# Hybrid block: nine units' low limbs by ScalarE and adding transfers, and eleven convolution taps from TensorE to VectorE

## What is computed

```python
proj = h @ w_in                                    # 1024 -> 2560
q, k, v, u, gate = split(proj)                     # five times 512
a_out = merge_heads(stick_breaking_attention(q, k, v))   # 8 heads of 64
c = u * sigmoid(gate)                              # 512 channels
c = causal_depthwise_conv(c, dw_w, dw_b)           # y_t = sum_k w_k x_(t-30+k) + b, 31 taps
c = silu(layer_norm(c, ln_g, ln_b))
m = concatenate([a_out, c]) @ w_out                # 1024 -> 1024
```

## Time and profile before

| | us |
|---|---|
| median of 3 runs | 1420.3 |
| lowest and highest | 1419.64, 1420.34 |
| span of the profiled execution | 1417.5 |
| PE (matmul) busy in the span | 1404.2 |
| VectorE busy | 940.8 |
| ScalarE busy | 723.2 |
| POOL busy | 150.7 |

### The profile page before, as it was taken

The page is one execution under the profiler, slowest core; times in us unless marked ns, Lnnn a source line. Parts: engine busy times, 40 slices in busy tenths (PEclk is TensorE's granted clock), DMA queues, the critical chain, the costliest instruction groups (busy, mean ns, idle before and its releaser), DMA issues.

```text
span 1417.5 us, 19077 instructions
## 1 busy us (share of the span) xinstructions
PE 1404.2 (99%) x7339; PEld 1149.0 (81%) x7339; DVE 940.8 (66%) x1294; ACT 723.2 (51%) x1042; POOL 150.7 (11%) x232
## 2 busy tenths in 40 slices
PE   9999999999999999999999999999999999999998
PEld 7888888688888888888878888888877788888886
DVE  6666667886676667665786857755568666765544
ACT  6444455564443445543755645446556644654442
POOL 1600010010000000000172100000552110000000
PEclk9999999999999999999999999999999999999999
DMA  9686765256876778868544688763945355565551
GB/s 317 199 252 201 260 203 205 68 177 199 259 243 206 235 233 259 252 216 264 181 144 163 202 205 265 250 211 125 247 154 194 119 178 179 163 209 184 201 193 61
DMA packets 236346, 286.15 MB, mean 202 GB/s; under 512 B 37028, under 2 KB 160720, under 8 KB 236256
## 3 DMA queue, kind: packets, MB, share of 16 engines
q1 hardware_dynamic: 235856, 284.63, 63.1%
q10 hardware_dynamic: 400, 0.31, 0.1%
HBM read 280.70 MB, written 4.20 MB: 201 GB/s over the span
## 4 chain that ended last, share of the span: by engine, by line
PE 95%; DVE 2%; issue 1%; ACT 1%; DMA 0%; SPq 0%; POOL 0%; POOLq 0%; ACTq 0%
PE ps L583 30%; PE ps L586 29%; PE ps L584 29%; PE pst L790 1%; PE pst L949 1%; DVE wlo L475 1%; PE pst L1225 1%; PE ps L1172 0%; DMA raw<-in_ffn_w_in_dram 0%; ACT whi L466 0%; PE pst L1539 0%; PE pst L2112 0%; PE ps L1209 0%; PE ps L1689 0%; PE pst L2321 0%
## 5 line engine op out<-in xcount | busy, mean ns | idle before, releaser
L475 DVE TENSOR_TENSOR wlo<-raw,whi 128x1024 fp32r<-128x1024 f32 (+2 forms) x474 | 564.2, 1224 | 252.3 <-ACT whi L466 250.7
L466 ACT ACTIVATE whi<-raw 128x1024 fp32r<-128x1024 f32 (+2 forms) x474 | 472.3, 1040 | 233.7 <-PE ps L586 94.0
L583 PE MATMUL ps<-whi,xh 128*128 128x512 f32 (+2 forms) x1438 | 563.9, 392 | 1.8 <-ACT xh L829 0.8
L584 PE MATMUL ps<-wlo,xh 128*128 128x512 f32 (+2 forms) x1438 | 553.6, 385 | 0.0
L586 PE MATMUL ps<-whi,xl 128*128 128x512 f32 (+2 forms) x1438 | 545.1, 385 | 0.0
L583 PEld LDWEIGHTS ps<-whi,xh 128*128 128x128 f32 x1438 | 270.0, 188 | 61.9 <-issue 4.7
L586 PEld LDWEIGHTS ps<-whi,xl 128*128 128x128 f32 x1438 | 270.0, 188 | 54.9
L584 PEld LDWEIGHTS ps<-wlo,xh 128*128 128x128 f32 x1438 | 270.2, 188 | 51.0
L583 PE MATMUL ps<-whi,gh 128*128 128x512 f32 x440 | 172.0, 391 | 0.0
L584 PE MATMUL ps<-wlo,gh 128*128 128x512 f32 x440 | 171.2, 389 | 0.0
L586 PE MATMUL ps<-whi,gl 128*128 128x512 f32 x440 | 153.4, 389 | 0.0
(11 more groups left out here) (272 smaller groups left out, 894.2 us busy)
## 6 DMA issues: line engine op xcount, KB each, us to landing
raw<-in_ffn_w_in_dram SPq DMA_DIRECT2D x174, 512.0 KB, 5.4
raw<-in_ffn_w_out_dram SPq DMA_DIRECT2D x40, 1024.0 KB, 5.8
raw<-in_w_in_dram SPq DMA_DIRECT2D x26, 1024.0 KB, 5.1
adat<-in_w_ada_dram SPq DMA_DIRECT2D x96, 256.0 KB, 3.1
raw<-in_w_ffn_gate_dram SPq DMA_DIRECT2D x22, 512.0 KB, 4.1
raw<-in_w_ffn_up_dram SPq DMA_DIRECT2D x22, 512.0 KB, 5.1
raw<-in_hyb_w_in_dram SPq DMA_DIRECT2D x10, 1024.0 KB, 5.2
raw<-in_gla_w_in_dram SPq DMA_DIRECT2D x10, 1024.0 KB, 5.1
```

What stands on the lines that cost most here:

```text
L466: e.activation(split_of(whi, j), raw_of(j), ACT.Copy).then_inc(*whi_made.up(j))
L475: e.tensor_tensor(split_of(wlo, j), raw_of(j), split_of(whi, j).bitcast(F32), ALU.subtract).then_inc(*wlo_made.up(j))
L583: e.matmul(ps[:, 0:n], a, whi_of(j, k), start=first and k == 0, stop=False)
L584: last = e.matmul(ps[:, 0:n], a, wlo_of(j, k), start=False, stop=False)
```

## The change

Units 5 to 13 of the hybrid stage (subs +10 to +27, 18 subs) are "soft". For them VectorE no longer makes the low limb. ScalarE writes the high limb as before and then the same value negated into `wlo` (a second activation with scale -1); POOL waits for that and issues a transfer that reads the same weights from DRAM again and adds them to `wlo`. TensorE and the loads of SP wait for that transfer (`s_lo`) instead of `wlo_made`. TensorE's taps are now the 31 of block 3, VectorE's the 93 of blocks 0 to 2; the added sum of block 2 is gone, and the copy, the join and the final read of the crossed quadrants are 256 columns wide instead of 512. The counts in the hand-written orders change with it.

```diff
+        soft = [*range(U0[1] + 5, U0[2])]
+        def lo_ready(j):
+            return s_lo[j % NSPL].at(j) if subs[j][0] in soft else wlo_made.at(j)
...
             if i >= NRAW:
-                e.wait_ge(*wlo_made.at(last_sub[i - NRAW]))
+                if i - NRAW in soft:
+                    e.wait_ge(*lo_ready(first_sub[i - NRAW]))
+                e.wait_ge(*lo_ready(last_sub[i - NRAW]))
...
                 e.activation(split_of(whi, j), raw_of(j), ACT.Copy).then_inc(*whi_made.up(j))
+                if u in soft:
+                    e.activation(split_of(wlo, j), raw_of(j), ACT.Copy, scale=-1.0).then_inc(*neg_made.up(j))
...
-                e.wait_ge(*whi_made.at(j))
-                e.tensor_tensor(split_of(wlo, j), raw_of(j), split_of(whi, j).bitcast(F32), ALU.subtract
-                                ).then_inc(*wlo_made.up(j))
+                if u not in soft:
+                    e.wait_ge(*whi_made.at(j))
+                    e.tensor_tensor(split_of(wlo, j), raw_of(j), split_of(whi, j).bitcast(F32), ALU.subtract
+                                    ).then_inc(*wlo_made.up(j))
...
+        def pool_lo(e, st):
+            for j in range(J0[st], J0[st + 1]):
+                u, k, m, n = subs[j]
+                if u in soft:
+                    srcs = plan[u][0]
+                    e.wait_ge(*neg_made.at(j))
+                    if len(srcs) == 1:
+                        e.dma_start(split_of(wlo, j), srcs[0][0][:, k:k + m, :], accum_op=ALU.add
+                                    ).then_inc(*s_lo[j % NSPL].up(j))
...
             if tok == 0:
-                e.wait_ge(*wlo_made.at(j))
+                e.wait_ge(*lo_ready(j))
...
-        NT = 20
-        PE_TAPS = [(2, k) for k in range(NT, 31)] + [(3, k) for k in range(31)]
-        TAPS = [(b, k) for k in range(31) for b in range(3) if b < 2 or k < NT]
+        PE_TAPS = [(3, k) for k in range(31)]
+        TAPS = [(b, k) for k in range(31) for b in range(3)]
...
-                t = e.matmul(tb.of("conv")[q, :], ident[p, p], hid[1][p, 0:512], start=False, stop=True,
+                t = e.matmul(tb.of("conv")[q, 0:256], ident[p, p], hid[1][p, 0:256], start=False, stop=True,
...
-            e.activation(hid[1][:, 0:512], tb.of("convx")[:, :], ACT.Copy).then_inc(*convx_made.up())
+            e.activation(hid[1][:, 0:256], tb.of("convx")[:, 0:256], ACT.Copy).then_inc(*convx_made.up())
...
             pool_open(e, 1)
+            pool_lo(e, 1)
             pool_open(e, 2)
```

More of the change, by code:

```diff
@@ L171, in program @@
         s_out_act = sig("s_out_act", 16)
+        s_lo = [sig(f"s_lo{i}", 16) for i in range(NSPL)]
+        neg_made = sig("neg_made")
         whi_made = sig("whi_made")
@@ L482, in split_lo @@
                         ada_sum(e, ada_summed[u])
+        def pool_lo(e, st):
[7 more added lines that the diff above has]
+                                    ).then_inc(*s_lo[j % NSPL].up(j))
+                    else:
+                        e.dma_start(split_of(wlo, j), raw_of(j), accum_op=ALU.add).then_inc(*s_lo[j % NSPL].up(j))
         def ada_add(e, c, k):
@@ L1059, in program @@
         tap_made = sig("tap_made")
-        taps_joined = sig("taps_joined")
         scored = sig("scored")
@@ L1215, in pe_taps @@
                 if i == 0:
-                    for name, last in ((("conv",), [(taps_joined,), (conv_out,)]), (("convx",), [(convx_made,)])):
+                    for name, last in ((("conv",), [(conv_out,)]), (("convx",), [(convx_made,)])):
                         tb.next(name, *last)
@@ L1224, in pe_taps @@
                     q = slice(64 - p.start, P - p.start) if i % 2 else p
-                    t = e.matmul(ps[q, (b - 2) * 256:(b - 1) * 256], diag[p, i * 64:(i + 1) * 64], cx_of(b, k)[p, :],
+                    t = e.matmul(ps[q, 0:256], diag[p, i * 64:(i + 1) * 64], cx_of(b, k)[p, :],
                                  start=i < 2, stop=i % 2 == 1 and k >= 29, skip_group_check=True)
@@ L1261, in pair @@
                     step(e, hd)
-            pe_taps(e, PE_TAPS[0:10])
+            pe_taps(e, PE_TAPS[0:8])
             pair(pe_weights, 0)
-            pe_taps(e, PE_TAPS[10:18])
+            pe_taps(e, PE_TAPS[8:14])
             pair(pe_weights, 1)
@@ L1267, in pe_hyb @@
             pe_scores(e, 2)
-            pe_taps(e, PE_TAPS[18:24])
+            pe_taps(e, PE_TAPS[14:18])
             pair(pe_values, 1)
             pe_scores(e, 3)
-            pe_taps(e, PE_TAPS[24:30])
+            pe_taps(e, PE_TAPS[18:22])
             pair(pe_weights, 2)
-            pe_taps(e, PE_TAPS[30:36])
+            pe_taps(e, PE_TAPS[22:26])
             pair(pe_weights, 3)
-            pe_taps(e, PE_TAPS[36:42])
+            pe_taps(e, PE_TAPS[26:31])
             pair(pe_values, 2)
@@ L1282, in norm @@
                     pe_total(e, "mean", y_of,
-                             lambda b: conv_out.at() if b == 3 else taps_joined.at() if b == 2
-                             else tap_made.at(b, 30), (y_centred, 3))
+                             lambda b: conv_out.at() if b == 3 else tap_made.at(b, 30),
+                             (y_centred, 3))
                 if i == 2:
@@ L1337, in act_hyb @@
             e.wait_ge(*conv_dot.at())
-            e.activation(hid[1][:, 0:512], tb.of("convx")[:, :], ACT.Copy).then_inc(*convx_made.up())
+            e.activation(hid[1][:, 0:256], tb.of("convx")[:, 0:256], ACT.Copy).then_inc(*convx_made.up())
             act_values(e, 2)
             e.wait_ge(*conv_sum.at())
-            e.activation(y_of(3), tb.of("conv")[:, 256:512], ACT.Identity, bias=vector("cb", 3)).then_inc(*conv_out.up())
+            e.activation(y_of(3), tb.of("conv")[:, 0:256], ACT.Identity, bias=vector("cb", 3)).then_inc(*conv_out.up())
             act_values(e, 3)
@@ L1396, in dve_hyb @@
                     if c > 2 or i >= 2:
-                        some(3)
+                        some(5)
             def logs(g):
@@ L1404, in dve_hyb @@
             logs(1)
-            some(20)
+            some(16)
             logs(2)
@@ L1410, in dve_hyb @@
             dve_values(e, 1)
-            some(11)
+            some(8)
             dve_values(e, 2)
             some(len(TAPS))
-            e.wait_ge(*tap_made.at(2, NT - 1))
-            e.wait_ge(*conv_out.at())
-            e.tensor_tensor(y_of(2), tb.of("conv")[:, 0:256], y_of(2), ALU.add).then_inc(*taps_joined.up())
             dve_values(e, 3)
```

## The result

The changed kernel takes 1434.05 us (median; 1434.02 to 1434.19), beside 1420.26 us before: a ratio of 1.0098, 95% interval 1.0084 to 1.0112. It is slower, as forecast, but by 13.8 us and not by 3.9. The profiled spans differ by 14.7 us (1417.5 and 1432.2): what lies around the span is 1.8 us in all four executions of the changed kernel, where the forecast took over the 2.8 us of the kernel before.

The account below looks back on a forecast made before the run. PE's matmul count and whatever makes PE wait bound the kernel. Taps and join -2.8, DVE free sooner -0.1, stall +4.7, clock +2.1 give +3.9 us: 1424.2 us, range 1419.3 to 1428.5.

Parts of the forecast that it names:

- PE's gain: Convolution taps and join on PE: 44 fewer tap matmuls save 2.37 us, the narrower join 0.42, 2.8 us in all.
- VectorE: Last taps before the layer norm's first total: done near 281.5 us, in time for PE at 281.6; cost 0, bound 1.0.
- sub +27: In w_out, the negated value is ready only 1.3 us before PE begins this sub, so PE stalls 4.7 us (1.8 to 7.7).
- L: Time for POOL to issue an adding transfer and for it to land: 1.0 + 5.0 = 6.0 us, bounds 3.1 and 9.
- the clock: After the 4.7 us stall, PE's granted clock falls to half rate for about 4 us, losing 2.1 us (bounds 0 and 4).
- Rival (a): The stall before sub +27 comes without a fall of the clock: +1.8 us, 1422.1 us; chance 0.24.
- room for 9 MB more: Hybrid stage: DMA shares of 0.53, 0.16 and 0.22 in three stretches leave space for the added reads of weights.
- no other wait of PE over 0.5 us: Sign of being right: from 215 us to the 4.7 us wait before sub +27, PE has no other wait this long.
- ScalarE's own cost at 0: A second activation per soft sub, 0.97 us each on ScalarE, delays nothing PE needs, so it costs 0.
- (c): Slow transfer, adding at a lower rate than copying: L = 8.5 us, stall 7.2 us, clock down, +6.4 us, 1426.7 us; chance 0.18.
- (b): Quick transfer, adding costs nothing: L = 4.1 us, stall 2.8 us, clock stays, -0.1 us, 1420.2 us; chance 0.15.
- (d): The new chain of negated value and adding transfer is hidden after all, so PE's gain stands: 1417.4 us; chance 0.06.

Follow-up runs that it names:

- the taps alone: Changed kernel with no soft unit: VectorE makes all low limbs as before and does the 93 taps as well; 1416.12 us, ratio 0.9974.
- the last unit alone: Changed kernel with only one soft unit, the last (subs +26 and +27); 1423.20 us, ratio 1.0021.
- the copying kernel: Changed kernel whose eighteen POOL transfers copy the weights over the negated values and add nothing, so its output differs; 1420.72 us, ratio 1.0007.
- three late units: Changed kernel with only three soft units, subs +20 to +25, whose low limbs are needed latest; 1416.37 us, ratio 0.9978.

## Why the prediction was wrong

**Right: PE's gain.** Forecast 2.8 us off PE and 0.1 beside it; the marked stretches give 2.8, and the taps alone shorten the profiled span by 3.1 us (1417.5 to 1414.4). The medians differ by 3.8 us, with an interval of 2.3 to 5.1 us about it; part of that lies around the span.

**Right: VectorE.** The last taps were to end near 281.5 us with PE at the total at 281.6; in the kernel with the taps alone, 281.5 and 281.49.

**Right: sub +27.** L alone was to be 6.0 us, and was 5.8; the wait was to be 4.7 us, and was 4.7 in the changed kernel and 4.7 alone. POOL's part is 1.20 us an issue, where I took 1.0; the two small errors in L (POOL's part too low, the rest too high) cancel in part. Taking that unit out gave 6.0 us.

**Right: the clock.** It fell, for 3.4 us where about 4 were forecast, at a price of 1.9 us in the profiled executions of the changed kernel and of the one with the last unit alone, against 2.1. Rival (a) is out. In all traces here PE waits ten times for 3.2 to 6.0 us, and each time the granted clock goes to 0.50, five times for 3.4 us and five times for 6.8 us. The shortest is the 3.2 us in the copying kernel, where the clock was 0.50 from 302 to 304 us. Waits of up to 1.7 us in mid-run did not bring it down; none lay between.

**Wrong: L as one number, and "room for 9 MB more".** The step that failed is the comparison of one L (6.0, bound 9) with each sub's room of 7.5 us and more, together with the sentence that the late loads "all land before ACT comes to them". L was 7.8 to 13.6 us for the first six transfers. The load of sub +16 went out 9.3 us later than before, where at most 5 were forecast, and took 13.3 us; it came at 241.5 us, and ScalarE had been ready for it since 232.2. I had read the DMA share as a mean of 42 us (0.53 in the earlier trace rows) and let it grow by "no more than a half"; it grew to 1.00 in that stretch, and from 0.16 to 0.93 in the next. A price in engine time was not in the sum at all. It could have been set up: a load of 512 KB takes 26 us of engine time by the page, reading the old values makes it up to twice that, 3.3 us of all 16 engines (measured 3.0), and ScalarE hands over a sub every 1.9 us. A queue that gets 3 us of work every 1.9 us grows. That was a cheap sum, and it says where the delay begins. The missing terms are 0.3 + 8.4 us among the chunks and 2.5 us between taps and join, 11.2 us in all. The forecast's sign of being right, no other wait of PE over 0.5 us, failed with 5.1, 1.0 and 0.8 us. In the medians 1.0 us of the error is hidden by luck, as the 2.8 us around the span were 1.8.

**ScalarE's own cost at 0: right by itself, but not with late loads.** The second activations cost nothing measurable in the kernel with three late units (1416.37 against 1416.12 us). But the order on ScalarE carries a late load over to the scores, which the forecast had not priced: a wait of 7.9 us for a load of w_out put its first work on the scores at 265.9 us, 0.2 us before PE's first tap (6.9 us before it with the taps alone, 249.9 and 256.8), and PE then waited 1.5 us for `mb`, which is made from them.

**The rivals.** (c), the slow transfer, had the right sign of the error, but it gave L = 8.5 us to every transfer. It was not the rate of one that was slow, but the sum of six. (b) needed a landing in 4.1 us and (d) no wait at sub +27; neither came.

Left open: how the engines share their time between a load and an adding transfer that are under way at once. The runs show the landing times and the sum, not the order inside. Open too is why the time around the span is 1.8 us with the new taps and 1.8 to 3.1 with the old.

## What to carry to other kernels

Give a new transfer three prices: its time alone, its time on the transfer engines, and the pace at which it is issued; if the second is longer than the third, its latency is that of a growing queue, and every load beside it pays. Here 3.0 and 2.8 us for all 16 engines (adding, from DRAM and from SBUF) at a pace of some 2 us made the stall, and 1.8 us (copying) did not. Look at the DMA engines in the few microseconds where the new work falls, not in the stage, and at both columns, share and GB/s: a full share with few bytes is the bad sign. When an engine is relieved, first see whether it had room: here the relief cost 18 us and was not needed.

## What the runs showed of the hardware

- A transfer that adds 512 KB to SBUF takes 48 us of engine time in all (3.0 us of 16 engines) against 29 for a copy issued by POOL in the same places and 26 for as many bytes loaded by SP. It lands 5.8 us after issue when alone, against 4.1 to 4.4 for the copy. By the fit in the Trainium skill ("DMA: Bandwidth & Descriptors", section Anatomy of one DMA — SWDGE (gpsimd) path) a copy of that size takes 3.2 us, an estimate; the shortest here was 4.1 us, and the measurement decides.
- POOL needs 1.20 us to issue one adding transfer (1.39 us for the first), 0.71 us for the copy and 0.87 us for adding from SBUF.
- The share of the 16 engines was 1.07 from 220 to 245 us both with adding and with copying transfers, at 255 and 336 GB/s.
- TensorE's granted clock fell to 0.50 at each of ten waits of 3.2 to 6.0 us, for 3.4 us in five and for 6.8 us in the other five. After the wait of 4.7 us before sub +27 the price was 1.9 us, with 3.4 us at half clock.
- Loads released sooner, beside adding transfers, made the kernel slower by 1.8 us: 1435.85 against 1434.05 us.
